# Queries of the first head for 128 tokens at a time, eviction by ScalarE, and value rows two heads behind

## The reference, cut to what matters

```python
def chunk(zc):                               # 128 tokens of z = rmsnorm(h) * g
    q = (zc @ peer_wq).reshape(128, 8, 2, 128)
    s1 = einsum('chd,hkd->chk', q[:, :, 0], k1); s2 = einsum('chd,hkd->chk', q[:, :, 1], k2)
    v1, i1 = top_k(s1, 16); v2, i2 = top_k(s2, 16)
    cand = v1[..., :, None] + v2[..., None, :]           # 16 x 16 sums
    top_s, top_pos = top_k(cand, 16); expert = index pairs of top_pos
    gate = softmax(top_s)
    act = gelu(einsum('chkd,cd->chk', take(peer_u, expert), zc))
    return einsum('chk,chkd->cd', gate * act, take(peer_v, expert))
```

## Time and profile before

| what | value |
|---|---|
| median of 3 runs | 2817.71 us (2816.95 to 2819.15) |
| the profiled execution, its own time | 2813.53 us |
| its span | 2811.6 us |
| mean granted TensorE clock | 0.976 |
| PE, DVE, ACT, POOL busy, share of the span | 85%, 62%, 28%, 19% |
| DMA: moved in all, of it by the rows' queue (q0) | 798.92 MB, 536.90 MB |
| GB/s in most slices from 1550 us on | 421 or 422 |

### The profile page before, as it was taken

The page is one execution under the profiler, slowest core; times in us unless marked ns, Lnnn a source line. Parts: engine busy times, 40 slices in busy tenths (PEclk is TensorE's granted clock), DMA queues, the critical chain, the costliest instruction groups (busy, mean ns, idle before and its releaser), DMA issues.

```text
span 2811.6 us, 29260 instructions
## 1 busy us (share of the span) xinstructions
PE 2384.8 (85%) x10874; PEld 1692.4 (60%) x10874; DVE 1748.5 (62%) x2554; ACT 782.2 (28%) x1151; POOL 520.3 (19%) x594
## 2 busy tenths in 40 slices
PE   8998899999999999899899857777777777777776
PEld 8986677888888888799788722222222222222222
DVE  6975547665666566677656995555655555555444
ACT  5423555443444344545430101001010110111010
POOL 0000000000000000100012453333333333333341
PEclk9998899999999999999999989999999999999999
DMA  7643254556555655544588999999999999999997
GB/s 223 185 99 119 74 168 148 190 183 194 181 193 180 193 180 168 176 150 150 164 255 305 421 420 422 422 421 421 422 421 421 422 421 422 421 421 421 421 422 326
DMA packets 339901, 798.92 MB, mean 284 GB/s; under 512 B 23313, under 2 KB 270699, under 8 KB 273771
## 3 DMA queue, kind: packets, MB, share of 16 engines
q0 software_dynamic: 73728, 536.90, 45.9%
q1 hardware_dynamic: 266091, 260.96, 29.3%
HBM read 795.72 MB, written 2.10 MB: 284 GB/s over the span
## 4 chain that ended last, share of the span: by engine, by line
DMA 37%; PE 13%; DVE 7%; issue 1%; POOL 1%; ACT 1%; DVEq 0%; POOLq 0%; PEldq 0%; ACTq 0%
DMA row<-in_peer_v,expert 30%; DMA row<-in_peer_u,expert 6%; DVE row L2145 4%; PE pl L798 3%; PE pl L1143 3%; PE pl L805 3%; PE pl L1082 1%; PE pl L801 1%; PE pl L802 1%; POOL row L709 1%; DVE wlo L1649 1%; DMA raw<-in_w_out 0%; ACT whi L1170 0%; DVE sq_r L2165 0%; DVE l_xc L2031 0%
## 5 line engine op out<-in xcount | busy, mean ns | idle before, releaser
L1143 PE MATMUL pl<-row,diag 128*128 128x512 f32 x1856 | 860.1, 607 | 332.3 <-DMA row<-in_peer_v,expert 327.2
L2145 DVE CUSTOM_DVE_ANT_0 row<-row,pg 128x2048 f32<-128x2048 f32 x256 | 581.6, 2286 | 444.9 <-DMA row<-in_peer_u,expert 443.5
L1143 PEld LDWEIGHTS pl<-row,diag 128*128 128x128 f32 x1856 | 337.7, 191 | 854.7 <-issue 456.5
L1649 DVE TENSOR_TENSOR wlo<-raw,whi 128x1024 fp32r<-128x1024 f32 (+1 forms) x436 | 517.1, 1207 | 378.3 <-ACT whi L1170 375.9
L1170 ACT ACTIVATE whi<-raw 128x1024 fp32r<-128x1024 f32 (+1 forms) x436 | 443.6, 1039 | 420.9 <-PE pl L805 401.7
L798 PE MATMUL pl<-x_split,whi 128*128 128x512 f32 x1888 | 477.6, 395 | 13.0 <-DVE x_split L1657 7.5
L798 PEld LDWEIGHTS pl<-x_split,whi 128*128 128x128 f32 x1888 | 341.5, 190 | 76.5 <-issue 9.2
L805 PE MATMUL pl<-x_split,wlo 128*128 128x256 f32 x2656 | 373.2, 284 | 6.1 <-DVE wlo L1649 6.1
L805 PEld LDWEIGHTS pl<-x_split,wlo 128*128 128x128 f32 x2656 | 358.6, 192 | 25.7 <-DVE wlo L1649 7.1
L709 POOL DMA_INDIRECT row<-in_peer_u,expert x256 | 240.7, 940 | 634.9 <-PE pl L1143 500.0
L1562 ACT ACTIVATE diag<-ident,dots 128x128 f32<-128x128 f32 x232 | 90.8, 399 | 887.4 <-PE pl L1143 861.0
(11 more groups left out here) (312 smaller groups left out, 1545.9 us busy)
## 6 DMA issues: line engine op xcount, KB each, us to landing
raw<-in_w_in SPq DMA_DIRECT2D x50, 1024.0 KB, 5.4
raw<-in_w_gate SPq DMA_DIRECT2D x44, 1024.0 KB, 5.1
raw<-in_w_up SPq DMA_DIRECT2D x44, 1024.0 KB, 5.1
raw<-in_w_out SPq DMA_DIRECT2D x32, 1024.0 KB, 5.5
raw<-in_w_down SPq DMA_DIRECT2D x32, 1024.0 KB, 5.4
wq<-in_peer_wq SPq DMA_DIRECT2D x16, 1024.0 KB, 11.2
raw<-in_w_down SPq DMA_DIRECT2D x16, 768.0 KB, 4.6
raw<-in_w_ukv SPq DMA_DIRECT2D x4, 1024.0 KB, 5.1
```

What stands on the lines that cost most here:

```text
L1143: last = mm(pl[q], diag[:, (at - 1) % 4, :], row[b][:, q * 512:(q + 1) * 512], start=(t == 1 and n == 0 and k == 0), stop=last_row, skip_g ...
L1649: V.tensor_tensor(wlo[:, n % 4, 0:k, :], w[:, :, f, :], whi[:, n % 4, 0:k, :].bitcast(F32), ALU.subtract)\
L2145: V.tensor_tensor_reduce(row[b][:], row[b][:], z_tok[:], 1.0, 0.0, ALU.mult, ALU.add, dots[:, at:at + 1])\
```

## The change

LAG goes from 3 to 2. The first head's queries, scores and selection are made for the first 128 tokens alone, then those of the other 128. The first block's expert numbers come out 8 at a time, and GpSimd may issue the first 8 rows after the first 8 of them. ScalarE takes the queries out of PSUM with a plain copy, in place of VectorE; the factor `rstd` moves into `gate_exp`. Both halves of a head's weights (heads 1 to 7) share a semaphore, so a head's first matmul waits for both. In the first block best_keys and choose stand after rows 8 and 10. In `residual` the weights' low parts are made after steps 2 and 4.

```diff
-LAG = 3
+LAG = 2
...
-        wq_in = [sem(f"wq_in{m}") for m in range(2 * PH)]
+        wq_in = [sem(f"wq_in0{m}") for m in range(2)]
+        wq_in += [s for s in [sem(f"wq_in{n}") for n in range(1, PH)] for _ in range(2)]
...
-                if table == "u" and k == 0:
+                if j == 0:
+                    pool.wait_ge(sel_first, 1)
+                elif (table == "u" and k == 0) or j == 8:
                     pool.wait_ge(sel_ready, t * PH + n + 1)
...
-            def queries(n, halves=(0, 1)):
+            def queries(n, halves=(0, 1), tokens=range(TT), done=wq_used):
-                bank = pl[n % 2]
+                bank, cols, width = pl[n % 2], tokens[0] * P, len(tokens) * P
...
-                    pe.wait_ge(wq_in[2 * n + half], 16)
+                    pe.wait_ge(wq_in[2 * n + half], 32 if n else 16)
...
-            queries(0, (0,))
+            queries(0, (0,), (0,), q0_done)
             wide_total("n2")
-            queries(0, (1,))
-            peer_scores(0)
+            queries(0, (1,), (0,), q0_done)
+            peer_scores(0, (0,))
...
+            token_rows(0)
+            token_rows(1)
+            queries(0, tokens=(1,))
             queries(1)
             pe.wait_ge(tok_r, 8)
+            peer_scores(0, (1,))
             peer_scores(1)
...
+            def query_copy(n, tokens=range(TT), done=wq_used, ready=wq_ready):
+                act.wait_ge(done, 1 if done is q0_done else n + 1)
+                if n >= 2:
+                    act.wait_ge(sc_done, n)
+                c = slice(tokens[0] * P, (tokens[-1] + 1) * P)
+                copy(qh[:, n % 2, :, c], pl[n % 2].rearrange("p (f s) -> p f s", f=2)[:, :, c]).then_inc(ready, 1)
...
-                activation(g, g, ACT.Exp).then_inc(sel_exp, 1)
+                activation(g, g, ACT.Exp, scale=small[:, 56 + t:57 + t]).then_inc(sel_exp, 1)
...
-            score_copy(0)
+            query_copy(0, (0,), q0_done, q0_ready)
+            score_copy(0, (0,))
...
-            for n in range(1, PH):
-                score_copy(n)
+            query_copy(0, (1,))
+            query_copy(1)
+            score_copy(0, (1,))
+            score_copy(1)
+            query_copy(2)
+            for n in range(3, PH):
+                query_copy(n)
+                score_copy(n - 1)
+            score_copy(PH - 1)
...
-                weights_lo(unit, piece, halves=(0,))
                 dve.wait_ge(gained, 8 * turn)
...
-                    if k == 3:
-                        weights_lo(unit, piece, halves=(1,))
+                    if k in (2, 4):
+                        weights_lo(unit, piece, halves=(k // 2 - 1,))
...
-            choose(0, 0)
+            link(V.max(ctop[:, 0:8], cand[:]))
+            V.max_index(cpos[:, 0:8], ctop[:, 0:8], cand[:])
+            link(V.match_replace(cand2[:], ctop[:, 0:8], cand[:], NEG))
+            experts(0, 8, [work[:, m, :].rearrange("p (k j) -> p k j", k=8) for m in range(2)], sel_first)
+            link(V.max(ctop[:, 8:16], cand2[:]))
...
+            experts(8, 16, [work[:, m, :].rearrange("p (k j) -> p k j", k=8) for m in range(2)], sel_ready)
...
-            EVICT = {(0, 1): 1, (0, 4): 2, (0, 9): 3, (0, 15): 4, (1, 3): 5, (1, 9): 6, (1, 14): 7}
...
-                    if k == 3 and i + 1 < 2 * PH:
+                    if k == (3 if i else 8) and i + 1 < 2 * PH:
                         best_keys(*divmod(i + 1, PH))
-                    if k == 6 and i + 1 < 2 * PH:
+                    if k == (6 if i else 10) and i + 1 < 2 * PH:
                         choose(*divmod(i + 1, PH))
-                    if (i, k) in EVICT:
-                        queries(EVICT[i, k])
```

More of the change, by code:

```diff
@@ L417, in build @@
         wq_ready = sem("wq_ready")
-        wq_in = [sem(f"wq_in{m}") for m in range(2 * PH)]
+        wq_in = [sem(f"wq_in0{m}") for m in range(2)]
+        wq_in += [s for s in [sem(f"wq_in{n}") for n in range(1, PH)] for _ in range(2)]
         wq_used = sem("wq_used")
+        q0_done = sem("q0_done")
+        q0_ready = sem("q0_ready")
+        sel_first = sem("sel_first")
         sc_done = sem("sc_done")
@@ L1069, in _ @@
             pe.wait_ge(z_scaled, 8)
-            def queries(n, halves=(0, 1)):
-                bank = pl[n % 2]
+            def queries(n, halves=(0, 1), tokens=range(TT), done=wq_used):
+                bank, cols, width = pl[n % 2], tokens[0] * P, len(tokens) * P
                 for half in halves:
-                    if half == 0:
+                    if half == 0 and tokens[0] == 0:
                         pe.wait_ge(wq_ready, n + 1)
                     w = wq[2 * n + half]
-                    pe.wait_ge(wq_in[2 * n + half], 16)
+                    pe.wait_ge(wq_in[2 * n + half], 32 if n else 16)
@@ L1079, in queries @@
                     for t in range(KU):
                         for f in range(2):
-                            first = half == 0 and t == 0 and f == 0
-                            last = mm(bank[:, f * S:(f + 1) * S], w[:, t, f, :], mix[:, half * KU + t, :], start=first,
+                            first = half == 0 and t == 0 and f == 0 and tokens[0] == 0
+                            last = mm(bank[:, f * S + cols:f * S + cols + width], w[:, t, f, :],
+                                      mix[:, half * KU + t, cols:cols + width], start=first,
@@ L1083, in queries, with peer_scores @@
                                       stop=(half == 1 and t == KU - 1), skip_group_check=True)
                     if half == 1:
-                        last.then_inc(wq_used, 1)
-            def peer_scores(n):
-                pe.wait_ge(wq_ready, n + 3)
+                        last.then_inc(done, 1)
+            def peer_scores(n, tokens=range(TT)):
+                if n == 0 and tokens[0] == 0:
+                    pe.wait_ge(q0_ready, 1)
+                else:
+                    pe.wait_ge(wq_ready, n + 3)
@@ L1090, in peer_scores @@
                 if n >= 2:
                     pe.wait_ge(sc_ready, 2 * (n - 1))
[L1093 to L1096, removed]
-                last.then_inc(sc_done, 1)
-            queries(0, (0,))
+                for t in tokens:
+                    for half in range(2):
+                        m = 2 * t + half
+                        last = mm(pl[2 + n % 2][:, m * P:(m + 1) * P], qh[:, n % 2, half, t * P:(t + 1) * P],
+                                  keysT[:, half * PH + n, :], start=True, stop=True)
@@ new lines, in peer_scores, with token_rows @@
+                last.then_inc(sc_done, 1)
+            def token_rows(t):
+                pe.wait_ge(norm_inv, NI["n2"] + 1)
+                for m in range(4 * t, 4 * t + 4):
+                    f4 = m % 4
+                    if m == 4:
+                        pe.wait_ge(rstd_tok, 1)
+                    elif m == 5:
+                        pe.wait_ge(sc_ready, 1)
+                    elif m >= 6:
+                        pe.wait_ge(tok_r, m - 1)
+                    bank = pg[f4] if t == 0 else pl[3 - m % 2]
+                    for f in range(4):
+                        last = nc.tensor.transpose(bank[:, f * P:(f + 1) * P],
+                                                   res[:, f4 * 4 + f, t * P:(t + 1) * P], ident[:])
+                    last.then_inc(tok_T, 1)
@@ L1532, in _, with score_copy @@
             norm_root(NI["n2"])
-            def score_copy(n):
-                act.wait_ge(sc_done, n + 1)
+            def query_copy(n, tokens=range(TT), done=wq_used, ready=wq_ready):
[4 more added lines that the diff above has]
+                copy(qh[:, n % 2, :, c], pl[n % 2].rearrange("p (f s) -> p f s", f=2)[:, :, c]).then_inc(ready, 1)
+            def score_copy(n, tokens=range(TT)):
+                act.wait_ge(sc_done, 1 if n == 0 and tokens[0] == 0 else n + 2)
                 bank = four(pl[2 + n % 2])
-                for t in range(TT):
+                for t in tokens:
                     copy(sc[t][:, n], bank[:, 2 * t:2 * t + 2]).then_inc(sc_ready, 1)
@@ L2156, in sum_row @@
                     .then_inc(row_summed, 1)
[L2158 to L2166, removed]
             def row_weights(pair):
@@ L2192, in final_rows, with experts @@
                         .then_inc(fin_out, 1)
-            queries(0)
-            best_keys(0, 0)
-            choose(0, 0)
+            def experts(n_first, n_last, halves, done):
+                m = slice(n_first, n_last)
+                ci = cpos[:, m].bitcast(I32)
+                V.tensor_scalar(cposi[:, 0, m], ci, 4, None, ALU.logical_shift_right)
+                link(V.tensor_scalar(cposi[:, 1, m], ci, 15, None, ALU.bitwise_and))
+                link(V.tensor_copy(cposf[:, :, m], cposi[:, :, m]))
+                full = [P, n_last - n_first, TOPK]
+                for half in range(2):
+                    last = V.tensor_tensor(halves[half], wide(cposf[:, half, m], 2, full),
+                                           iota16[:].unsqueeze(1).broadcast_to(full), ALU.is_equal)
+                link(last)
```

(14 more changed lines are left out.)

## The result

The changed kernel takes **2833.03 us** (median of five runs, 2832.22 to 2841.01) against 2819.15 for the kernel before (five runs, 2816.95 to 2824.76), a ratio of 1.0057 with a 95% interval from 1.0036 to 1.0077. It is slower by some 0.6%; forecast were 2838 and a range from 2813 to 2846. The two profiled executions, 2833.03 and 2813.53, lie 19.5 us apart, where the sum had 20.1.

A forecast was written before the change was run, and what follows sets the result against it. Expert rows were taken as bound by DMA bytes. +18.9 us (earlier start, two late loads, dry spell) and +1.2 for the norms gave +20.1 on 2813.5, 2833.6; with 4.2 for the median, 2838 us, range 2813 to 2846.

The forecast's parts named there:

- Earlier start: First head: shorter query records, copies, scores and selection bring the first row issue 9.2 us earlier (bounds 7.8 and 9.7).
- Loads 10 and 11: Weight loads waiting for `wq_used` at 1 now move behind rows: two MB more in the bound stretch, +5.0 us.
- The weights starve: Six queued weight loads get 0.05 MB/us beside rows; load 15, for head 7, is in only at 1608 (1604.6 to 1613.1).
- The gap of the row queue: Row queue empty once before row 16's bytes, 2.6 us (1.1 to 3.2), letting weights move at 0.32 MB/us.
- LAG = 2 makes this a wait of the rows: Row 42 needs value row 33's buffer, so GpSimd stands until head 7's late chain ends; row 42 used at 1641.6.
- The shared semaphore: Head's first matmul waits for both weight halves: cost 0, as both are there or the second is missing.
- The hole and what follows: DMA engines dry about 25 us after 1613.3; 469 rows at 2.51 us follow row 42, ending at 2818.8, +18.9.
- The norms: Low parts of the weights made later in `residual`: +0.6 hidden after the mixer, +1.2 us (0 to 1.9) after the FFN.
- The level: Median of the runs taken as 4.2 us above the profiled execution, so 2833.6 becomes 2838.
- The rule against the turns: Skill's whole-packet turns would give weights 9 KB or more per 7.3 KB of rows, loads in by about 1530; chance 0.03.

The follow-up runs named there:

- experiment 5: Changed kernel, VectorE waiting after product row 4 of the first block for head 2's queries, evicting nothing: 2817.09 us, 0.9993 of the kernel before.
- experiment 9: Changed kernel with the VectorE wait of experiment 5 and the old place of the weights_lo calls in residual: 2815.24 us, 0.9985 of the kernel before.
- experiment 3: Changed kernel with LAG = 3 again, all else as changed: 2836.86 us, 1.0068 of the kernel before.
- experiment 1: Kernel before with only the two weights_lo calls in residual moved to after steps 2 and 4: 2822.08 us, 1.0009 of the kernel before.

## Why the prediction was right, and where not

**Earlier start: right.** From the first query record to the first row issue it was 27.51 us before and is 18.12 now, 9.4 less where 9.2 was forecast. Both figures are of profiles in which the first 32 query records ran at a granted clock of 1.00. In seven of the twelve profiles they ran at 0.57 to 0.61, after the same 2.27 us of idle time; there it is 29.1 to 29.2 before and 19.7 to 19.8 in the changed kernels, again 9.4. The fp32 products of 128 columns take 0.12 us each, as the transposes do (3.81 / 32).

**Loads 10 and 11 at +5.0: not measured alone**, but the sums agree. -9.2 + 5.0 and the measured 2.5 of the norms give -1.7 for experiment 5 (measured: -2), and -4.2 without the norms for experiment 9 (measured: 0.9985, -4.2). Each measured figure has an interval of 2.5 us to either side, so a term of 3 or of 7 would agree as well.

**The weights starve: right, its size by two errors that nearly cancel.** TensorE was forecast to restart at 1609.1 and, with everything 3.7 later, at 1612.8; it did at 1607.90. The gap of the row queue was longer than the 2.6 us put down: 1.62 MB of weights in 1540 to 1546, at 0.35 when alone and 0.05 beside rows, is 4.4 us. Row 16 was issued at 1541.66, 2.4 later than forecast with the shift, and the first row bytes came at 1546.3, 4.65 us on, beyond the 4.2 of my upper bound. The gap alone, 4.4 us at 0.35 in place of 2.6 at 0.32, is 0.7 MB, and would have brought the load in some 12 us earlier (an estimate, at 0.05 MB/us). But the end of a load is slow. The weight queue of this kernel from 1580 to 1600 and from 1600 to 1610:

```profile
q1 hardware_dynamic: 854, 0.86, 12.8%
...
q1 hardware_dynamic: 51, 0.05, 1.5%
```

99% of the six loads are in by 1600. The last 0.05 MB, 51 records that were left on a few of the engines, took until 1607.8, one turn at a time. I had counted a load as a sum of bytes; it ends with its slowest engine. So 12 us too early and 8 us too late are left as 4 to 5 us too early, and that the load came near the forecast is luck in part.

**"LAG = 2 makes this a wait of the rows": the step that failed.** The chain itself is right, link by link: head 7 at 1607.90, scores 1624.61, gelu 1630.64, value row 1631.66, row 42 issued 1635.63, each 4 to 5 us earlier than its forecast with the shift, as the load was. But its gate is one of two behind the same gates on ScalarE. The sentence "VectorE waits in `row_weights` meanwhile" took the other one as without effect. With LAG = 2 it is: row 42 takes the buffer of value row 33 and row 43 that of product row 34, which VectorE had used before it stood. With LAG = 3 row 34 stands behind VectorE's wait, and experiment 3 shows that this alone holds row 43 for 29.6 us. So the chain was right and the blame on LAG wrong. The diff's LAG is innocent: 1.0002 alone, and 1.0068 with it put back in the changed kernel.

**The shared semaphore: put at nothing without a reason that holds.** The prediction took the wait for both halves as free, "both are there, or the second is what is missing". The second was missing, but the first half was in at 1586.7 and TensorE was free. With a semaphore for each half, as before, TensorE could have worked off 32 of head 7's 64 records by about 1595, and only the other 32 would have stood behind the late load. By the 16.87 us that the 64 took, that is an estimate of 7 to 8 us off the hole, getting on for half of what the change lost. The sum came out all the same, since it put all 64 records behind the load. No run here tests it.

**The hole and what follows: right.** Dry from about 1619 to 1637, 18 us, where "about 25 us" was forecast. The rows up to 41 held out till 1619 and not 1613.3: 3.7 of it is the shift and 1.8 the longer gap. The end of the hole, which sets the time, came where it was forecast, and this too is luck in part: the load was 4 to 5 us earlier than its forecast with the shift, and the shift itself was 3.7 where the norms' term had 1.2. Row 42 was used at 1641.33, and 469 rows later the last value row starts at 2819.39: 2.512 us each, where 2.51 was put down.

**The norms: mechanism right, size off.** The term was +1.2 from ScalarE's queue. At the FFN's norm TensorE's idle time before the last split grew from 0.95 to 2.04 us, 1.1, as forecast (0.95 in all seven profiles with the old norms, 2.01 to 2.10 in the five with the new). Not forecast was the clock. After the idle time it was granted at 0.69 and 0.74, where before it was 1.00 (the windows of experiment 1 show the same, but five of the seven profiles with the old norms dip there too); at the first norm, put down as hidden, TensorE's sum came 1.4 us later for it (451.18 against 449.77). Profiled the term came to +3.7, part of it scatter of the dense layers; in the medians it is 2.5 (0 to 5).

**The level.** I added the 4.2 us by which the profiled execution of before lay under its median. The profiled execution of the changed kernel lies on its median, so the sum over profiles (19.5) is larger than that of the medians (13.9 to 16). This is the 5 us by which 2838 is too high.

**The rule against the turns: the measurement decides, but not by the counts.** The counts are equal (893 records of weights against 895 of rows in 1510 to 1528), and the prediction took this as turns of one record. But turns of ten records on both queues would give equal counts too, and the same bytes: it had set the longer turn on the weights' side alone, and the loads starve by either. The order of the records settles it. The last weight records of head 7 start at 1605.81, 1606.17, 1606.53 and 1606.88, some 0.36 us apart: one row record (0.31 us) and one weight record (0.05 us) by turns. The Trainium skill ("DMA: Bandwidth & Descriptors", section "Queues, rings and completion order") has an engine drain a packet of typically 9 to 17 descriptors before it switches. With a record for a descriptor, this stretch shows turns of one.

## What to carry to other kernels

In these runs two DMA queues shared the engines by turns of one record, and the one with small records got bytes in the ratio of the record sizes, 1 to 7, for as long as the other never ran empty. A wait that you remove from the big queue's feeder may have been the only time in which the small one was served: before you call a stall a cost, ask which transfers lived in it, and if there are any, put a wait where their consumer needs them. And where a late event stops a pipeline, list every engine that stands behind it; undoing the one gate that opened last need not help. A semaphore shared by two loads costs nothing only while both come in time.

## What the runs showed of the hardware

- A stretch in which only the weight queue had work moved 348 to 350 GB/s with records of 1.0 KB; rows of 8 KB run at 421.
- The last 0.8% of six queued loads took 8 of some 110 us; 51 records were left, the last of them 0.36 us apart.
- An indirect DMA issued while the weight queue was busy and the row queue all but empty brought its first row bytes after 4.6 to 4.7 us in three kernels (changed 1541.66 to 1546.31, before 1529.79 to 1534.45, experiment 5 1527.40 to 1532.03). With both queues empty it was 1.6 to 1.8 us (1635.63 to 1637.26, 1492.47 to 1494.26, before 1498.13 to 1499.92).
- An idle time of TensorE that was 0.7 us longer (1.73 against 1.00, first norm) cost 1.6 us more in the 16 records behind it (1.70 and 3.13 us against 1.22 and 2.00), at a granted clock of 0.72 to 0.86 in five profiles against 1.00 in the seven without the edit.
- The same idle time need not bring the same clock: after 2.27 us ahead of the first query record it was 1.00 over the next 4 us in five profiles and 0.57 to 0.61 in seven. The four with the new norms among the changed kernels are all of the first kind, the four with the old norms of the second. The reason stays open.
